# Output products of the state space part: the four summands in the outer loop, the four groups of 32 channels in the inner one

## The chip, the cores and the metric

The kernel runs on one core of a Trainium2 chip. The core has a matrix engine (TensorE, in the rows PE for the products and PEld for the loads of their stationary operand), a vector engine (VectorE, DVE), an activation engine (ScalarE, ACT), GpSimd (POOL) and SyncE (SP), whose queue starts the transfers from memory. Each engine runs its own list of instructions in order, and they meet through semaphores. PSUM, into which TensorE writes, has 8 banks of 128 partitions by 512 numbers of 32 bits. The metric is the device time of one execution in microseconds (us), as the median of several runs.

## What is computed

A layer with three mixers side by side (a diagonal state space part called S5, attention, retention), an output product, and then a layer of experts picked by keys. The change touches the end of the S5 part alone: the output `y`, a real product with the two halves of the complex state.

```python
def s5_mixer(u, lam_re, lam_im, log_dt, b_re, b_im, c_re, c_im, d_skip, w_glu):
    ...
    _, _, st_r, st_i = lax.associative_scan(_ssm_combine, (a_r, a_i, bu_r, bu_i), axis=1)
    y = (jnp.einsum('bsgp,ghp->bsgh', st_r, c_re.astype(jnp.float32))
         - jnp.einsum('bsgp,ghp->bsgh', st_i, c_im.astype(jnp.float32))
         + uf * d_skip.astype(jnp.float32).reshape(S5_NGROUPS, S5_GROUP))
    y = jax.nn.gelu(y.reshape(bsz, s, S5_CH))
    y = y * jax.nn.sigmoid(y @ w_glu.astype(jnp.float32))
    return y.astype(u.dtype)
```

There are 256 tokens (s), 16 groups (g) of 16 channels (h) with 64 states (p) each, so 256 channels and 1024 states. All numbers are of 32 bits.

## The kernel before

**Tiling of the S5 part.** Two groups with 64 states each fill the 128 partitions, so the 1024 states are 8 tiles `jj` of 128 states by 256 tokens. A tile feeds only its own 32 channels. Four tiles (`j` = 0 to 3) make up the 128 channels of one half `c` of the channels, and `c` runs over 0 and 1.

**The four summands.** The state of a tile is kept rotated: VectorE multiplies the two scanned arrays `zr` and `zi` with the cosines `pc` and the sines `pS`, and never adds the products up. So each tile has four arrays of 128 states by 256 tokens: `pc` (by then zr times cosine), `zi` (zi times sine), `xr` (zi times cosine) and `zr` (zr times sine). TensorE adds them up in PSUM by four products, with the real matrix `c_s[:, 0]`, its negative `c_neg[:, 0]`, and twice the negative of the imaginary one, `c_neg[:, 1]`.

**The products (line 521).** One product has a stationary operand of 128 states by 32 channels and a moving one of 128 states by 256 tokens. It writes 32 partitions of bank 6: partitions 32j to 32j + 31, columns 256c to 256c + 255. In the trace its form is "128*32 128x256". The four products of a tile accumulate on the same 32 partitions (`start` with the first, `stop` with the last). There are 2 by 4 by 4 = 32 of them. All operands are plain 32 bit numbers, and the trace has two records of every such product, so 64 records for these 32.

**Order before.** For each `c` the loop over `j` is outside and that over the four summands inside: four products in a row go to the same 32 partitions, then the next four go to the next 32.

**What stands around it in TensorE's list.** Ahead: the attention products at lines 500 and 509 and the last projection (`project(5, t)`, line 408). Behind: 8 transposes of the retention operands (line 530), 8 of the attention weights (line 538), the retention scores (551, 556), the gate's product (562) and more transposes and small products up to line 602. Then 16 products that only keep the engine busy (`keep_warm`, line 400), the transposes of the mixed result (392) and the output product by slices (426 to 428).

**Who waits for the end of line 521.** The last product sets `y_psum`, on which VectorE waits at line 911 (it adds the direct term), ScalarE's GELU (1254) stands behind that. ScalarE waits at line 1250 for the transposes of line 530, which stand behind line 521 in TensorE's own list. GpSimd has nothing to do until ScalarE has rounded the first slices of the output weights (1147), which comes after the whole mixing part.

**Other line for comparison.** `drive` (line 417) computes the inputs of the scans with products of another shape, "32*128 32x256": 32 partitions of input, 128 of output, a bank of its own for each `j`. There the loop over `j` is inside already.

Of the kernel before, what the change touches and what calls it, by code (L numbers as in the profile page):

```python
# [27 lines left out]
S = 256  # L28
# [87 lines left out]
def build(nc, x, w_in, vecs, consts, rots, decay, mask, s5_b, s5_c, w_glu, w_out, w_q, keys, u_t, v, out, spill):  # L116
    with ExitStack() as ctx:
# [24 lines left out]
        ps = ctx.enter_context(nc.psum_tensor("ps", [P, 8, 512], F32))  # L142
# [12 lines left out]
        def take(n):  # L155
            a = cursor[0]
            cursor[0] += n
            assert cursor[0] <= S * NKEY, cursor[0]
            return arena[:, a:a + n]
# [13 lines left out]
        pc = r3(take(S5_T * S), S5_T)  # L173
        zr, zi = (r3(take(S5_T * S), S5_T) for _ in range(2))
        squares = zr.rearrange("p j t -> p (j t)")
        xr = xn.rearrange("p t d -> p (t d)").rearrange("p (j t) -> p j t", j=S5_T)
# [30 lines left out]
        c_s = rawf[:, 2816:2816 + 512].rearrange("p (r j c) -> p r j c", r=2, j=S5_T)  # L207
        bb = rawf[:, 3328:3328 + 512].rearrange("p (r j c) -> p r j c", r=2, j=S5_T)
        c_neg = b_s
# [171 lines left out]
        def _(pe):  # L381
# [40 lines left out]
            def halves_product(dst, pairs, first, last):  # L422

                for i, (s_hi, s_lo, m_hi, m_lo) in enumerate(pairs):
                    end = last and i == len(pairs) - 1
                    pe.matmul(dst, s_hi, m_hi, start=first and i == 0, stop=False)  # L426
                    pe.matmul(dst, s_hi, m_lo, start=False, stop=False)  # L427
                    mm = pe.matmul(dst, s_lo, m_hi, start=False, stop=end)  # L428
                return mm
# [33 lines left out]
            for c in range(S5_C):  # L463
                for t in range(TT):
                    mm = pe.transpose(ps[:, 5, c * S + t * P:c * S + (t + 1) * P], u_tok[:, t, c * P:(c + 1) * P], ident)
            mm.then_inc(uT_psum, 1)
            pe.wait_ge(bb_ready, 1)
            for r in range(2):
                for c in range(S5_C):
                    mm = pe.transpose(ps[:, 6, (r * 2 + c) * P:(r * 2 + c + 1) * P],  # L470
                                      bb[:, r, 4 * c:4 * c + 4, :].rearrange("p j c -> p (j c)"), ident)
# [16 lines left out]
            for a in range(2):  # L488
                for h in range(4):
                    for t in range(TT):  # L490
                        mm = pe.transpose(ps[:, 4 + 2 * a + h // 2, (h % 2) * S + t * P:(h % 2) * S + (t + 1) * P],
                                          qk[:, t, a * MW + h * P:a * MW + (h + 1) * P], ident)
# [4 lines left out]
            for h in range(4):  # L497
                for o_ in range(2):
                    r = slice(HD * o_, HD * (o_ + 1))
                    mm = pe.matmul(ps[:, 4 + 2 * o_ + h // 2, (h % 2) * S:(h % 2 + 1) * S], mqT[r, h, P:S], mkT[r, h, :],  # L500
                                   start=True, stop=True)
# [4 lines left out]
            for h in range(4):  # L506
                for o_ in range(2):
                    r = slice(HD * o_, HD * (o_ + 1))
                    mm = pe.matmul(ps[:, 4 + o_, h * P:(h + 1) * P], mqT[r, h, 0:P], mkT[r, h, 0:P], start=True, stop=True)
# [3 lines left out]
            pe.wait_ge(c_ready, 1)  # L513
            for c in range(S5_C):
                pe.wait_ge(states_ready, c + 1)
                for j in range(4):
                    jj = 4 * c + j
                    parts = ((c_s[:, 0, jj, :], pc[:, jj]), (c_neg[:, 0, jj, :], zi[:, jj]),
                             (c_neg[:, 1, jj, :], xr[:, jj]), (c_neg[:, 1, jj, :], zr[:, jj]))
                    for n, (w, st) in enumerate(parts):  # L520
                        mm = pe.matmul(ps[32 * j:32 * j + 32, 6, c * S:(c + 1) * S], w, st,  # L521
                                       start=(n == 0), stop=(n == len(parts) - 1))
            mm.then_inc(y_psum, 1)

# [2 lines left out]
            for a in range(2):  # L527
                for h in range(2):
                    for t in range(TT):
                        mm = pe.transpose(ps[:, 2 + a, h * S + t * P:h * S + (t + 1) * P],  # L530
                                          ret[:, t, a * RW + h * P:a * RW + (h + 1) * P], ident)
# [21 lines left out]
            for h in range(2):  # L553
                for o_ in range(2):
                    r = slice(HD * o_, HD * (o_ + 1))
                    mm = pe.matmul(ps[:, 2 + o_, h * P:(h + 1) * P], rkT[r, h, P:S], rqT[r, h, P:S], start=True, stop=True)
# [3 lines left out]
            for m in range(S5_C):  # L560
                for c in range(S5_C):
                    mm = pe.matmul(ps[:, 7, m * S:(m + 1) * S], glu_s[:, c, m * P:(m + 1) * P], uT[:, c, :],
                                   start=(c == 0), stop=(c == S5_C - 1))
# [3 lines left out]
            for t in range(TT):  # L567
                for c in range(S5_C):
                    mm = pe.transpose(ps[:, 6, t * S5_CH + c * P:t * S5_CH + (c + 1) * P], uT[:, c, t * P:(t + 1) * P], ident)
# [8 lines left out]
            for h in range(RH):  # L578
# [4 lines left out]
                mm = pe.matmul(o1, rP1[:, h, :], ret[:, 1, vc], start=False, stop=True)  # L583
# [7 lines left out]
            for h in range(MH):  # L591
                g = 4 * (h % 2) + h // 2
                c = slice(h * HD, (h + 1) * HD)
                mm = pe.matmul(ps[:, 4, c], att0[:, g // 4, g % 4, :], mv[:, 0, c], start=True, stop=True)
# [3 lines left out]
            for h in range(MH):  # L598
                g = 4 * (h % 2) + h // 2
                c = slice(h * HD, (h + 1) * HD)  # L600
                pe.matmul(ps[:, 5, c], att1[:, g, 0:P], mv[:, 0, c], start=True, stop=False)
                mm = pe.matmul(ps[:, 5, c], att1[:, g, P:S], mv[:, 1, c], start=False, stop=True)
# [6 lines left out]
            for n in range(2):  # L609
                for k in range(KC):  # L610
# [4 lines left out]
                    for t in range(TT):  # L615
                        r = slice(t * P, (t + 1) * P)
                        mm = halves_product(ps[:, 4 + 2 * n + t, :],
                                            [(h_hi[:, k, r], h_lo[:, k, r], w_hi[:, k % 4, :], w_lo[:, k % 4, :])],
                                            k == 0, k == KC - 1)
# [5 lines left out]
            for n in range(2):  # L625
                for k in range(KC):
# [4 lines left out]
                    for h in range(4):  # L631
                        c = slice(h * P, (h + 1) * P)
                        mm = halves_product(ps[:, 4 * (1 - n) + h, 0:S],
                                            [(w_hi[:, k % 4, c], w_lo[:, k % 4, c], h_hi[:, k, :], h_lo[:, k, :])],
                                            k == 0, k == KC - 1)
# [46 lines left out]
            for t in range(TT):  # L682
                for a in range(3):
                    mm = pe.transpose(ps[:, 4 + t, a * P:(a + 1) * P], rows[:, t, a, :], ident)
# [842 lines left out]
```

## Time and profile before

| | us |
|---|---|
| median of 3 runs | 970.44 |
| the three runs | 970.31, 970.44, 973.07 |
| the profiled execution, its own time | 970.3 |
| span in its trace | 968.5 |
| from the first record of line 521 to the first of line 530 | 8.10 |
| mean granted clock of TensorE | 0.986 |

The span runs from the first to the last instruction of the trace; the 1.8 us around it belong to the time of the run and not to the trace. Of an engine's busy time TensorE has 96%. The first 205 us hold the mixers and the projections, in which the engines take turns; the rest is the expert part, one loop over the up projections and one over the down projections.

### The profile page before, as it was taken

The page shows a single profiled execution, that of the slowest core. Times are in us where ns is not written, and L with a number is a line of the kernel's source. Part 1 is how long each engine was busy: PE and PEld are TensorE (multiplying, and loading weights), DVE is VectorE, ACT ScalarE, POOL GpSimd, SP SyncE. Part 2 cuts the span into 40 slices and gives each one's busy share as a digit, 9 for nine tenths or more (in the row PEclk, how much of TensorE's full clock was granted, in tenths as well). Part 3 has the DMA queues.
Part 4 walks back from the last instruction along what each step waited for, and adds up shares of the span by engine and source line. Part 5 has one row for each costly group of instructions (what it writes and reads, how often), then busy time and mean ns, then how long its engine had stood idle before and what let it go on. Part 6 is the DMA issues. An engine that isn't in the chain of part 4 may idle for free.

```text
span 968.5 us, 20031 instructions
## 1 busy us (share of the span) xinstructions
PE 926.8 (96%) x5920; PEld 828.8 (86%) x5920; DVE 692.5 (72%) x1496; ACT 528.8 (55%) x1044; POOL 447.8 (46%) x370
## 2 busy tenths in 40 slices
PE   5794999999999999999999999999999999999998
PEld 5553568899999999999999999988888888888886
DVE  7379534202999912688888887788888888888886
ACT  4622555555555455555555555655566555655553
POOL 1779606587888888777777777300000000000000
PEclk9897999999999999999999999999999999999999
DMA  9422222216666666565555555776767677777773
GB/s 332 160 104 87 87 87 90 108 45 217 200 231 225 230 230 208 206 199 194 193 196 194 200 190 194 234 245 239 247 238 243 231 246 236 248 238 244 243 234 134
DMA packets 67435, 191.45 MB, mean 198 GB/s; under 512 B 6480, under 2 KB 8272, under 8 KB 67408
## 3 DMA queue, kind: packets, MB, share of 16 engines
q1 hardware_dynamic: 67408, 191.11, 57.8%
q8 instruction: 15, 0.25, 0.1%
q14 instruction: 12, 0.10, 0.0%
HBM read 173.78 MB, written 17.30 MB: 197 GB/s over the span
## 4 chain that ended last, share of the span: by engine, by line
PE 70%; POOL 14%; issue 7%; DVE 5%; ACT 3%; DMA 0%; POOLq 0%; SPq 0%; DVEq 0%
PE ps L426 21%; PE ps L427 21%; PE ps L428 21%; POOL w_lo L1455 10%; PE ps L666 3%; POOL w_lo L1419 2%; DVE routing L737 2%; PE ps L408 1%; PE ps L521 1%; ACT w_hi L1147 1%; PE ps L392 1%; ACT h_hi L1154 0%; DMA xs<-in_x 0%; DVE small L737 0%; DVE route_t L737 0%
## 5 line engine op out<-in xcount | busy, mean ns | idle before, releaser
L1311 ACT ACTIVATE w_hi<-raw 128x512 fp32r<-128x512 f32 x512 | 308.4, 628 | 137.3 <-PE ps L428 136.2
L1455 POOL TENSOR_TENSOR w_lo<-raw,w_hi 128x512 fp32r<-128x512 f32 x256 | 327.0, 1298 | 81.2 <-ACT w_hi L1311 80.9
L426 PE MATMUL ps<-h_hi,w_hi 128*128 128x256 f32 x1088 | 308.5, 284 | 2.5 <-POOL w_lo L1455 1.1
L427 PE MATMUL ps<-h_lo,w_hi 128*128 128x256 f32 x1088 | 307.9, 283 | 0.0
L428 PE MATMUL ps<-h_hi,w_lo 128*128 128x256 f32 x1088 | 307.8, 283 | 0.0
L737 DVE TENSOR_TENSOR w_lo<-raw,w_hi 128x512 fp32r<-128x512 f32 x256 | 177.4, 693 | 56.9 <-ACT w_hi L1311 41.9
L426 PEld LDWEIGHTS ps<-h_hi,w_hi 128*128 128x128 f32 x1088 | 208.8, 192 | 3.3 <-POOL w_lo L1455 1.3
L427 PEld LDWEIGHTS ps<-h_lo,w_hi 128*128 128x128 f32 x1088 | 208.8, 192 | 0.0
L428 PEld LDWEIGHTS ps<-h_hi,w_lo 128*128 128x128 f32 x1088 | 208.8, 192 | 0.0
L426 PE MATMUL ps<-w_hi,hot_gate 128*128 128x512 f32 x512 | 199.2, 389 | 0.0
L427 PE MATMUL ps<-w_lo,hot_gate 128*128 128x512 f32 x512 | 199.2, 389 | 0.0
L428 PE MATMUL ps<-w_hi,hot_gate 128*128 128x512 f32 x512 | 199.2, 389 | 0.0
L1325 ACT ACTIVATE acts<-ps 128x256 f32<-128x256 f32 x128 | 49.0, 383 | 177.5 <-PE ps L428 177.4
L1419 POOL TENSOR_TENSOR w_lo<-routing,w_hi 128x512 fp32r<-128x512 f32 (+1 forms) x64 | 84.6, 1339 | 81.4 <-ACT w_hi L1147 79.4
L426 PEld LDWEIGHTS ps<-w_hi,hot_gate 128*128 128x128 f32 x512 | 96.1, 188 | 20.1
L427 PEld LDWEIGHTS ps<-w_lo,hot_gate 128*128 128x128 f32 x512 | 96.1, 188 | 19.9
L428 PEld LDWEIGHTS ps<-w_hi,hot_gate 128*128 128x128 f32 x512 | 96.1, 188 | 19.8
L1066 DVE SCALAR_TENSOR_TENSOR hot_gate<-ps,route_t 128x256 fp32r<-128x256 f32 x256 | 105.6, 474 | 0.0
L737 DVE TENSOR_TENSOR route_t<-acts,routing 128x256 f32<-128x256 f32 x128 | 81.3, 635 | 3.0 <-ACT acts L1325 2.1
L737 DVE TENSOR_TENSOR routing<-routing,ps 128x512 f32 (+2 forms) x66 | 48.6, 736 | 40.0 <-ACT routing L1331 40.0
L426 PE MATMUL ps<-w_hi,h_hi 128*128 128x512 f32 (+1 forms) x96 | 39.3, 409 | 18.2 <-POOL w_lo L1419 17.4
L737 DVE TENSOR_TENSOR hot_gate<-route_t,hot_gate 128x256 fp32r<-128x256 f32 x128 | 53.9, 421 | 3.4 <-ACT hot_gate L1369 3.4
(196 smaller groups left out, 885.2 us busy)
## 6 DMA issues: line engine op xcount, KB each, us to landing
raw<-in_u_t SPq DMA_DIRECT2D x128, 512.0 KB, 3.4
raw<-in_v SPq DMA_DIRECT2D x128, 512.0 KB, 3.4
act_spill<-acts SPq DMA_DIRECT2D x62, 256.0 KB, 2.1
acts<-act_spill SPq DMA_DIRECT2D x62, 256.0 KB, 3.4
routing<-in_w_in SPq DMA_DIRECT2D x5, 2048.0 KB, 9.3
routing<-in_w_out SPq DMA_DIRECT2D x2, 2048.0 KB, 8.2
routing<-in_w_q SPq DMA_DIRECT2D x2, 2048.0 KB, 7.7
xs<-in_x SPq DMA_DIRECT2D x2, 512.0 KB, 4.9
```

The source lines that it names most:

```text
L392: mm = pe.transpose(ps[:, k // 2, (k % 2) * S + t * P:(k % 2) * S + (t + 1) * P], src[:, t, k * P:(k + 1) * P], ident)
L408: mm = pe.matmul(ps[:, 2 * ((n - 1) % 2) + t, :], hT[:, k, t * P:(t + 1) * P], w[:, k, :], start=(k == 0), stop=(k == KC - 1))
L426: pe.matmul(dst, s_hi, m_hi, start=first and i == 0, stop=False)
L427: pe.matmul(dst, s_hi, m_lo, start=False, stop=False)
L428: mm = pe.matmul(dst, s_lo, m_hi, start=False, stop=end)
L666: mm = pe.matmul(ps[:, 4 + 2 * (s % 2) + q // 2, (q % 2) * 2 * NKEY:(q % 2 + 1) * 2 * NKEY], hot_j[:, s % 2, q, :], hot_gate[:, s % 2, q]. ...
L737: return V.tensor_tensor(out_, a, b, op)
L1066: ins = V.scalar_tensor_tensor(hot_gate[:, s % 2, q], iota_p.unsqueeze(1).to_broadcast([P, 2, NKEY]), route_t[:, 0, one], route_t[:, 2:4, ...
L1311: A.activation(w_hi[:, 2 * (s % 2) + h, :], raw[:, s, h * HALF:(h + 1) * HALF], ACT.Copy)\
L1325: A.activation(acts[:, s, :], ps[:, s % 2, 0:S], ACT.Gelu_apprx_tanh).then_inc(act_ready, 1)
L1419: G.tensor_tensor(w_lo[:, m % 4, 0:width], w_ring[n % W_SLOTS][:, k, 0:width], w_hi[:, m % 4, 0:width].bitcast(F32), ALU.subtract).then_in ...
L1455: G.tensor_tensor(w_lo[:, slot, :], raw[:, s, h * HALF:(h + 1) * HALF], w_hi[:, slot, :].bitcast(F32), ALU.subtract).then_inc(lo_ready, 1)
```

## The change

The two loops inside `c` change places. The arrays are sliced by tile in the call and not ahead of it; operands, shapes, places in PSUM, flags, semaphores and the number of products are the same, and each output still adds up its four summands in the same order.

```diff
             for c in range(S5_C):
                 pe.wait_ge(states_ready, c + 1)
-                for j in range(4):
-                    jj = 4 * c + j
-                    parts = ((c_s[:, 0, jj, :], pc[:, jj]), (c_neg[:, 0, jj, :], zi[:, jj]),
-                             (c_neg[:, 1, jj, :], xr[:, jj]), (c_neg[:, 1, jj, :], zr[:, jj]))
-                    for n, (w, st) in enumerate(parts):
-                        mm = pe.matmul(ps[32 * j:32 * j + 32, 6, c * S:(c + 1) * S], w, st,
+                parts = ((c_s[:, 0], pc), (c_neg[:, 0], zi), (c_neg[:, 1], xr), (c_neg[:, 1], zr))
+                for n, (w, st) in enumerate(parts):
+                    for j in range(4):
+                        mm = pe.matmul(ps[32 * j:32 * j + 32, 6, c * S:(c + 1) * S], w[:, 4 * c + j, :], st[:, 4 * c + j],
                                        start=(n == 0), stop=(n == len(parts) - 1))
             mm.then_inc(y_psum, 1)
```

TensorE's list before, from the last projection to the transposes behind the S5 products (a name in brackets is a semaphore that the row waits for; xN is a count of rows alike):

```order
L408 MATMUL ps<-routing 128x512 [waits hT_ready,proj_ready,weights_in2]
L408 MATMUL ps<-routing 128x512 x7
L521 MATMUL ps<-routing,raw 32x256 [waits states_ready,c_negated]
L521 MATMUL ps<-routing,raw 32x256 x15
L521 MATMUL ps<-routing,raw 32x256 [waits states_ready]
L521 MATMUL ps<-routing,raw 32x256 x15
L530 MATMUL ps<-con,routing 128x128 [waits proj_ready,ret_rotated_ready]
```

The same place in the changed kernel, where the lines behind the edit are two lower:

```order
L408 MATMUL ps<-routing 128x512 [waits hT_ready,proj_ready,weights_in2]
L408 MATMUL ps<-routing 128x512 x7
L519 MATMUL ps<-routing,raw 32x256 [waits states_ready,c_negated]
L519 MATMUL ps<-routing,raw 32x256 x15
L519 MATMUL ps<-routing,raw 32x256 [waits states_ready]
L519 MATMUL ps<-routing,raw 32x256 x15
L528 MATMUL ps<-con,routing 128x128 [waits proj_ready,ret_rotated_ready]
```

Nothing moved between engines or across another line or wait. Only within each sixteen the order differs, which these rows don't show since all sixteen read alike: before, the 32 output partitions of `j` came 0 0 0 0 1 1 1 1 2 2 2 2 3 3 3 3, now 0 1 2 3 four times over.

## Rows read from the trace of the kernel before

**Rows 1.** Page, sections 1 and 2: busy time, then tenths per fortieth of the span.
```profile
PE 926.8 (96%) x5920; PEld 828.8 (86%) x5920; DVE 692.5 (72%) x1496; ACT 528.8 (55%) x1044; POOL 447.8 (46%) x370
PE   5794999999999999999999999999999999999998
PEclk9897999999999999999999999999999999999999
```

**Rows 2.** Chain that ended last, 104.7 to 134.2 us: start, us, what ended last.
```profile
104.80 1.93 PE ps L500 x16
106.73 7.06 PE ps L408 x16
113.79 1.09 PE ps L509 x16
114.88 7.06 PE ps L408 x16
121.95 8.10 PE ps L521 x64
130.04 1.04 PE ps L530 x8
...
131.11 0.60 ACT routing L1250
```

**Rows 3.** Line 521: records, ns shortest/median/longest, first and last start; who waited.
```profile
L521 PEld LDWEIGHTS ps<-routing,raw x64: 106/110/110, 121.9 to 129.5; 128*32 128x32 f32 x64
L521 PE MATMUL ps<-routing,raw x64: 379/379/404, 121.9 to 129.7; 128*32 128x256 f32 x64
...
  DVE routing L911: 12.5, 1
```

**Rows 4.** Timeline, loads of line 521: start, us, count; the first four of one tile.
```profile
121.88 0.11 PEld L521 LDWEIGHTS ps<-routing,raw 128*32 128x32 f32 x1 [0.76 <-issue]
122.12 0.11 PEld L521 LDWEIGHTS ps<-routing,raw 128*32 128x32 f32 x1
122.33 0.11 PEld L521 LDWEIGHTS ps<-routing,raw 128*32 128x32 f32 x1
122.55 0.11 PEld L521 LDWEIGHTS ps<-routing,raw 128*32 128x32 f32 x1
```

**Rows 5.** The same timeline a little later: loads that overlap are merged.
```profile
122.77 0.11 PEld L521 LDWEIGHTS ps<-routing,raw 128*32 128x32 f32 x2
122.98 0.14 PEld L521 LDWEIGHTS ps<-routing,raw 128*32 128x32 f32 x2
123.20 0.14 PEld L521 LDWEIGHTS ps<-routing,raw 128*32 128x32 f32 x2
```

**Rows 6.** Line 417 (`j` inside already), first drive: start, us, what, count.
```profile
45.72 0.31 PEld L417 LDWEIGHTS ps<-routing,raw 32*128 32x128 f32 x8 [0.35 <-issue]
46.04 0.20 PEld L417 LDWEIGHTS ps<-routing,raw 32*128 32x128 f32 x4
46.26 0.20 PEld L417 LDWEIGHTS ps<-routing,raw 32*128 32x128 f32 x4
```

**Rows 7.** Waits from 121 to 131 us; timeline behind line 521.
```profile
DVE routing L911 <- PE ps L521: 12.5, 1, 12.5
...
129.98 0.33 PE L530 MATMUL ps<-con,routing 128*128 128x128 f32 x1
```

**Rows 8.** Timeline from 104 us: what ScalarE and GpSimd wait for.
```profile
113.91 0.74 POOL L1407 TENSOR_TENSOR routing<-routing 128x256 f32<-128x256 f32 x1
121.98 0.69 ACT L1210 ACTIVATE routing<-ps,small 128x512 f32<-128x512 f32 x1 [1.22 <-PE ps L408]
131.11 0.60 ACT L1250 ACTIVATE routing<-ps 128x512 f32<-128x512 f32 x1 [8.44 <-PE ps L530]
```

**Rows 9.** Windows: PE, PEld, DVE, ACT, POOL busy, granted clock, DMA share, GB/s.
```profile
81.30:84.70 3.40, 1.42 (x7) 0.84 (x5) 3.37 (x3) 1.26 (x2) 3.32 (x3) 1.00 0.87 329
84.70:98.35 13.65, 3.39 (x17) 3.42 (x17) 13.44 (x15) 0.00 (x0) 13.41 (x15) 0.50 0.00 0
125.70:129.10 3.40, 3.40 (x33) 2.02 (x30) 0.00 (x0) 0.00 (x0) 0.00 (x0) 1.00 0.98 369
135.90:139.30 3.40, 1.78 (x16) 1.51 (x15) 1.47 (x3) 3.36 (x5) 0.00 (x0) 1.00 0.00 0
```

## The prediction

> **What bounds the kernel now.** I read the page first: TensorE is busy 96% of the span and no other engine is near it [rows 1], so a shorter stretch of TensorE can count, if it is one that everything waits for. The chain that ended last says whether it is. Between 104.8 and 130.0 us it is nothing but TensorE, line after line, and the 64 records of line 521 are 8.10 us of it (121.95 to 130.04); behind them come the transposes of line 530 and then ScalarE's copy at line 1250 [rows 2]. Then I asked who stands still meanwhile. VectorE waits 12.5 us for line 521 [rows 7]. ScalarE ends its last piece at 121.98 + 0.69 = 122.67 us and waits 8.44 us for line 530 (it starts at 131.11), and GpSimd's last piece ended at 113.91 + 0.74 = 114.65 us [rows 8]. Over 125.7 to 129.1 us VectorE, ScalarE and GpSimd are at 0.00 busy [rows 9]. What line 530 waits for besides its place in the list, the rotated retention operands, is GpSimd's piece of 114.65 us. So nothing lies beside line 521 that would be late next, down to 122.67 us, and what it loses the rest of the kernel gets, as long as the rest runs as before.
>
> **How the 8.10 us come about.** The first loads of line 521 start at 121.88, 122.12, 122.33 and 122.55 us [rows 4]: 0.24 us after the first record of a tile, then 0.216 (a record of 256 columns). Those all go to the 32 output partitions of j = 0. At 122.77 us two loads start at once, and from then on loads come in pairs 0.03 us apart, a new pair after 0.215 us (122.98, 123.20), each pair over in 0.14 us [rows 5]. I read the second of a pair as that of j = 1, whose products start while those of j = 0 still run. One stream of 8 tiles with 8 records each would need 64 x 0.216 = 13.8 us; it took 8.10, so on average 13.8 / 8.10 = 1.7 groups of 32 partitions were at work at a time. With four products in a row for each group, only neighbours meet: the second half of one with the first half of the next.
>
> **The change, part by part.** It removes, adds and moves nothing but the order within each sixteen products; waits, records and places are the same.
>
> *What it costs in each group:* for one j there are 4 summands x 2 records x 2 halves c = 16 records. They have to follow each other at 0.216 us, since they accumulate on the same partitions, as before.
>
> *What goes away:* now four neighbouring products have four different j. Nothing of the trace shows four groups of output partitions at once. The nearest rows are two. One is line 521 itself, where two ran together and neither became slower (0.215 us from pair to pair, as for one alone) [rows 5]. The other is line 417, four groups of input partitions with j inside: 8 loads in 0.31 us, then 4 at 46.04 and 4 at 46.26 us, so four streams side by side with 0.22 us to a round, and the fourth load only 0.02 us behind the first (0.20 us for four loads of 0.18) [rows 6]. Bounds: at best all four run freely, 16 rounds; at worst they take turns. I take the first end, because line 521 already shows the same kind of stream twice at no cost, and line 417 that TensorE's list can feed four.
>
> *The sum:* first gap 0.24, 14 more of 0.216 = 3.02, so the last round starts 3.26 us after the first; 0.02 for the fourth stream; then as now to line 530: the last record of line 521 starts 0.3 us before it (129.7 against 129.98 [rows 3, 7]). Together 3.6 us in place of 8.10, a gain of **4.5 us**.
>
> *Both halves c.* The second half waits for states that VectorE had finished long before: it idles for 12.5 us up to the end of line 521, 130.04, so it was done at about 117.5 [rows 2, 7]. No new wait.
>
> *Feeding the list.* Four streams take a record every 0.054 us, where line 521 now takes one every 0.127 (8.10 / 64). While the projection runs for 7.06 us [rows 2] the products behind it can queue up, and line 417 took records at that rate, though only 16 of them [rows 6]. If the list ran dry and the second half went at the rate of now, it would take 32 x 0.127 = 4.1 us instead of 1.8, and the gain would be 2.2 us. That is the price of the cover being too short.
>
> *What then comes earlier.* Everything from line 530 on moves by the gain. The transfer of 2 MB that starts at 122 us (0.98 of the DMA engines, 369 GB/s up to 129) now runs beside transposes and ScalarE copies that came after it. Beside that same transfer line 521 did 30 loads in 3.4 us [rows 9], 0.113 us each, no slower than its mean, so I cost this at nothing. The profiled execution of before took 970.3 us around a span of 968.5, and the median is 970.44, so both stand for the same state; 970.4 less 4.5 is **965.9 us**.
>
> A rule of the Trainium skill speaks against this sum. "TensorE: Matmul & The Clock Gate", part 3 (Packing small matmuls), says that a weight load overlaps products in flight only where the two have different row groups; here all tiles use the same 128 rows. By that, line 521 would have no two streams, and the change could gain nothing. The trace disagrees already: loads of 0.11 us start at 122.12 and 122.33 us while records of 0.379 us run, and the round still is 0.216 us [rows 3 to 5]. The same part gives 2.38 times for three column tiles, an estimate by which the 13.8 us of records would be 5.8 us for three and less for four; it names the gain, but with another width.
>
> **Rivals.**
> - *Loads take turns* (that rule, as a mechanism of this kernel): each of the four loads of a round, 0.11 us, stops all streams. A round is 0.216 + 4 x 0.11 = 0.66 us, 16 of them 10.5, with 0.3 behind them 10.8 us: **973.1 us**, slower. Against it: rows 4 and 5, where loads cost nothing.
> - *A drain at each change of group.* Between line 408 and 521, or 521 and 530, TensorE changes its form and loses about 0.1 us (0.3 to the next record where 0.216 is usual). If every change of j cost that and kept streams apart, the 32 products would take 0.24 + 0.31 us each, 17.6 us in all: 9.5 us more, **979.9 us**. This decides as soon as a product costs over 8.10 / 32 = 0.253 us. For it: before, there are only 7 changes of j, now 31. Against: the changes that are there start 0.006 to 0.03 us after the record before [rows 5], no drain. I give both of these 4% together.
> - *Two streams at most.* What the trace shows is two. Then 32 rounds of 0.216 + 0.3 = 7.2 us, a gain of 0.9: **969.5 us**. Reading the moving operands could be the limit: four streams of 128 partitions read four times what line 417 reads. 8%, with the case that the order in the list isn't what sets the overlap.
> - *Three, or a list that runs dry:* 64 / 3 rounds + 0.3 = 4.9 us, a gain of 3.2 us, or 2.2 by the sum above: **967.2 to 968.2 us**. 10%.
> - *The clock.* TensorE's granted clock fell from 2.4 to 1.2 GHz at 84.7 us, after a stretch of 3.4 us with TensorE at 1.42 us busy, and stayed there for 13.65 us; with 1.78 of 3.4 us busy, in 135.9 to 139.3, it stayed at 2.4 [rows 9]. That thin stretch stays as it is, but comes 4.5 us earlier and closer behind the projection, with a shorter S5 part between. If the clock fell there for as long as at 84.7, TensorE's work would take up to 13.65 / 2 = 6.8 us more: 965.9 to **972.7 us**. 5%.
>
> **How the numbers follow.** Full overlap 73%, three streams or a dry list 10%, two streams or no effect 8%, the clock 5%, turns or drains 4%. The likeliest gives 965.9 us. For the range, the full case has some tenths of its own (the runs of before differ by 0.1 us, with one at +2.6), which sets 964.7 below. Above, it has to take in the three streams and the two, so 969.7; what lies outside is most of the clock's case and the slower ones, and runs that scatter. A measurement of this kernel can tell about 0.3% (2.9 us) from no change: faster then means under 967.5. That is the full case, a part of the three streams and little of the clock: 0.78. Slower, above 973.3, is the drain: 0.03. The rest is 0.19.
>
> **What would show it.** In the profile of the changed kernel the products should take about 3.6 us from their first record to the first transpose, with loads in fours every 0.216 us; VectorE's wait for them should be 8.0 instead of 12.5 us, and ScalarE's for line 530 3.9 instead of 8.4. Rounds of 0.43 us would say two streams, 0.29 three, 0.66 loads that take turns. Rounds of 0.216 first and slower ones in the second half would say that the list ran dry. If the products are that short and the time isn't 4.5 us lower, the windows from 130 to 205 us tell where it went: a granted clock of 0.50 in them, or a wait that was not there. The forecast is wrong if four streams of 128 partitions can't be read at once, which no row shows.

## The result: 965.9 us, and the 4.5 us are where they were looked for

The changed kernel takes 965.89 us (median of 6 runs, 965.31 to 966.08) against 970.40 (median of 6) for the kernel before. The ratio is 0.9946, with a 95% interval of 0.9931 to 0.9960: a gain of 0.4 to 0.7%. The profiled execution took 965.99 us around a span of 964.2, so 1.8 us lie around the span, as before.

The page of the changed kernel, sections 1 and 2, answers to [rows 1]:

```profile
PE 922.8 (96%) x5920; PEld 826.6 (86%) x5920; DVE 692.5 (72%) x1496; ACT 528.6 (55%) x1044; POOL 447.8 (46%) x370
PE   5794999999999999999999999999999999999998
PEclk9797999999999999999999999999999999999999
```

TensorE's products are busy for 4.0 us less and its loads for 2.2 us less; the other engines differ by 0.2 us at most. The chain that ended last, from 104.9 to 134 us (start, us, what ended last), answers to [rows 2]:

```profile
104.99 1.93 PE ps L500 x16
106.92 7.06 PE ps L408 x16
113.98 1.09 PE ps L509 x16
115.08 7.07 PE ps L408 x16
122.14 3.59 PE ps L519 x64
125.73 1.04 PE ps L528 x8
126.77 0.02 issue
126.79 0.60 ACT routing L1248
```

Each piece has its length of before, but for line 519 (521 before): 3.59 us in place of 8.10. What the line is made of, and the loads in the timeline (loads that overlap are merged, with their count), answer to [rows 3 to 5]:

```profile
L519 PEld LDWEIGHTS ps<-routing,raw x64: 106/110/111, 122.1 to 125.1; 128*32 128x32 f32 x64
L519 PE MATMUL ps<-routing,raw x64: 378/379/403, 122.1 to 125.4; 128*32 128x256 f32 x64
```

```profile
122.31 0.13 PEld L519 LDWEIGHTS ps<-routing,raw 128*32 128x32 f32 x4
122.53 0.13 PEld L519 LDWEIGHTS ps<-routing,raw 128*32 128x32 f32 x4
122.74 0.13 PEld L519 LDWEIGHTS ps<-routing,raw 128*32 128x32 f32 x4
```

A record is as long as before (0.379 us, of which the end is modelled by the profile, so the starts count for more), a round is 0.216 us as before, but now a round holds four loads, all within 0.13 us where one takes 0.11. Four streams of 128 partitions run side by side and none is slower for it.

Who waited, and for how long (engine and line, what it waited for, us in all, times, longest), answers to [rows 7, 8]:

```profile
DVE routing L909 <- PE ps L519: 8.1, 1, 8.1
...
ACT routing L1248 <- PE ps L528: 3.9, 1, 3.9
```

The span fell by 4.3 us and not by 4.5. The first piece of the chain, the transfer of the input, is the reason; the rows are the first of the chain from 0 to 36 us, of the kernel before and of the changed one:

```profile
1.67 4.50 DMA xs<-in_x
```

```profile
2.14 5.70 DMA xs<-in_x
```

It ended 1.7 us later (7.84 against 6.17), and of that 0.19 us were left where the mixers' last products begin: line 500 began at 104.99 against 104.80, and 4.51 - 0.19 = 4.32 us, which is the 968.5 - 964.2 of the spans. Behind line 519 nothing is given back: from there to the end of the loops the records of TensorE stand 4.30 to 4.32 us earlier all along.

### The profile page after: what moved, and what is told of

It reads as the page before. It is cut to its first block, busy times and chain, and to the rows that moved or that the text cites. A ratio compares the mean times of both kernels' runs of the same rounds, so it can differ in the third digit from the quotient of the medians.

```text
span 964.2 us, 20031 instructions
## 1 busy us (share of the span) xinstructions
PE 922.8 (96%) x5920; PEld 826.6 (86%) x5920; DVE 692.5 (72%) x1496; ACT 528.6 (55%) x1044; POOL 447.8 (46%) x370
## 4 chain that ended last, share of the span: by engine, by line
PE 70%; POOL 14%; issue 7%; DVE 5%; ACT 3%; DMA 1%; POOLq 0%; SPq 0%; DVEq 0%
PE ps L426 21%; PE ps L428 21%; PE ps L427 21%; POOL w_lo L1453 10%; PE ps L664 3%; POOL w_lo L1417 2%; DVE routing L735 2%; PE ps L408 1%; DMA xs<-in_x 1%; ACT w_hi L1145 1%; ACT h_hi L1152 0%; PE ps L519 0%; DVE small L735 0%; DVE route_t L735 0%; POOL routing L1437 0%
```

## Experiments

The question that the result leaves is why the old order had 1.7 groups at work, and what in general decides. The theory was formed on [rows 4, 5]: j = 1 began 0.89 us after j = 0, four records or two products later, so when the third product of j = 0 began to run and only its fourth was left to wait. So: TensorE takes products in the order of the list; each group of 32 output columns holds two of them, one that runs and one that waits; the first product that finds its group full holds up all behind it, of whatever group. All numbers below are of the stretch from the first product to the first transpose behind, as the chain gives it; the kernel before has 8.10 us there and the changed one 3.59. Each kernel computes the reference's outputs in full. The diffs are against the changed kernel, whose two loops go out in each of them but the last; `...` stands for lines left out, such as the product's call with the operands and places of before.

**Two summands of a group in a row.**

```diff
-                for n, (w, st) in enumerate(parts):
-                    for j in range(4):
+                for n, j in [(2 * a + b, j) for a in range(2) for j in range(4) for b in range(2)]:
+                    w, st = parts[n]
...
```

> The same 32 products, but two summands of one group of 32 channels in a row before the next group comes: 0 0 1 1 2 2 3 3, twice for each half. Theory: the matrix engine takes products in the order of its list, and a group of 32 output columns holds two of them, one that runs and one that waits; the first that finds its group full stops the list. Then two in a row are free, all four groups run at once, and the stretch up to the transposes is 3.6 us as with the new order, 966 us in all. Rival: a group only starts when its predecessor has half of its block behind it, so two streams at a time whatever the length of a block: 7.5 us and about 970 us.

The chain of this kernel:

```profile
125.10 3.66 PE ps L519 x64
```

3.66 us, and 966.08 us in all (median of 8; ratio 0.9951, 0.9938 to 0.9964). So it isn't needed that neighbours differ. The rival, by which this would have stayed with two streams (7.5 us), is out. So is a limit on how far ahead of the oldest unfinished product TensorE looks, whatever the group: the order of before would put it at three products (j = 1, the fifth, began with the third), and here the first product of j = 3 is the seventh in the list, and 3.66 us leave no room for it to wait. (The profiled execution of this kernel took 969.03 us; 3.0 us of it had been lost by 65.4 us, see the last section.)

**Three in a row, then one each.**

```diff
+                for n, j in [(n, j) for j in range(4) for n in range(3)] + [(3, j) for j in range(4)]:
...
```

> Three summands of a group in a row (000 111 222 333), then the fourth of each (0 1 2 3), for each half. Theory of two held per group: the third product stops the list for two records (0.43 us) in each block, and the stretch takes 5.3 to 5.5 us (worked out product by product with 0.216 us a record), 967.7 us in all. If a group held three products it would be 3.6 us, if one only 8.35 us. Rival of half a block: about 6.6 us.

```profile
121.72 5.51 PE ps L519 x64
```

and loads near its start (two places of the timeline; loads that overlap are merged, with their count):

```profile
121.65 0.14 PEld L519 LDWEIGHTS ps<-routing,raw 128*32 128x32 f32 x2 [0.76 <-issue]
...
122.11 0.14 PEld L519 LDWEIGHTS ps<-routing,raw 128*32 128x32 f32 x3
```

5.51 us for an expected 5.3 to 5.5, and 967.89 us in all (median of 5). At 122.11, 0.46 us after the start, three loads come at once: I read them as the next of j = 0 and the first two of j = 1. So the second group came in two records after the first here, and four records after it in the old order (0.89 us), in both when all products of j = 0 but the waiting one had begun. The third product in a row is the one that costs: a group that held three would have given 3.6 us, one that held one 8.35, and the rival of half a block 6.6. This run names the number two, and the old order agrees: counted in the same way, 0.216 us a record, it would take 10.9 us with one held and 4.8 with three, and it took 8.10.

**The new order in the first half of the channels only.**

```diff
+                order = [(n, j) for n in range(4) for j in range(4)] if c == 0 else [(n, j) for j in range(4) for n in range(4)]
+                for n, j in order:
...
```

> The new order for the first half of the channels, the order of before for the second. Theory of two held per group: 6.2 to 6.4 us for the stretch (16 us records of the second half staggered as before), so 1.8 us less than before, 968.6 us. Not half of the gain (5.85 us, 968.1 us), because the old order's cost lies in its blocks being staggered one behind the other and its last block is short of company in either kernel. Rival: the time is a sum of two independent halves, 5.85 us.

```profile
125.02 6.25 PE ps L520 x64
```

6.25 us for 6.2 to 6.4 by the theory, and 5.85 by a sum of two halves; 968.84 us in all (median of 10; ratio 0.9982, 0.9970 to 0.9994). Half of the edit brings 1.85 of the 4.51 us, as the last block of the old order ends alone in either kernel.

**Groups in pairs.**

```diff
+                for n, j in [(n, 2 * a + b) for a in range(2) for n in range(4) for b in range(2)]:
...
```

> Groups in pairs: all four summands for groups 0 and 1 by turns, then for groups 2 and 3, for each half. Theory of two held per group: the second pair starts once the fourth summand of the first pair is accepted, four records (0.86 us) after its start, so 4.5 to 4.7 us for the stretch and 966.9 us in all. Rival, two streams at most at any time by the hardware: 7.2 us, 969.5 us (this fell already with the changed kernel, which had four).

```profile
125.09 4.55 PE ps L519 x64
```

4.55 us for 4.5 to 4.7; 967.20 us in all. With this, six orders of the same 32 products gave 8.10, 6.25, 5.51, 4.55, 3.66 and 3.59 us, each within some 0.2 us of what the rule of two gives product by product (7.9, 6.2, 5.3, 4.5, 3.6, 3.6). What the rule lacks in the old order fits the first gap of a block, 0.24 us in place of 0.216 [rows 4], which is paid anew by each block. One thing these runs can't tell: every product is two records, so "two products" may as well be "four records".

**Four times the work.** This is for the step on which the prediction had least: whether the list can feed four streams once what queued up behind the projection is used.

```diff
-                for n, (w, st) in enumerate(parts):
-                    for j in range(4):
+                for n, j in [(n, j) for _ in range(4) for n in range(4) for j in range(4)]:
+                    w, st = parts[n]
...
```

> The new order with each sixteen products done four times over, the last time's result counting (128 products, 256 records). Theory, the list feeds four streams for as long as it must: 64 rounds of 0.216 us, 14.0 us for the stretch, 10.4 us more than the changed kernel, 976.3 us. Rival, the list runs dry once what queued up behind the projection is used: rounds longer than 0.216 us from some place on, at the old rate of 0.127 us a record up to 30 us for the stretch.

```profile
122.01 13.95 PE ps L519 x256
```

13.95 us, so 64 rounds of 0.216 us: in the trace each round starts 0.215 or 0.216 us after the one before (0.24 for the first), so 256 records at one in 0.054 us. The list never ran dry. The whole took 978.27 us (2 runs) and not 976.3: 2 us more than the stretch explains, which appear at the very end.

**Twice the loads for the same columns.** This is for the loads.

```diff
-                for n, (w, st) in enumerate(parts):
-                    for j in range(4):
...
+                for h in range(2):
+                    for n, (w, st) in enumerate(parts):
+                        for j in range(4):
+                            mm = pe.matmul(ps[32 * j:32 * j + 32, 6, c * S + h * P:c * S + (h + 1) * P], w[:, 4 * c + j, :],
+                                           st[:, 4 * c + j, h * P:(h + 1) * P], start=(n == 0), stop=(n == len(parts) - 1))
```

> The new order with each product cut in two of 128 tokens (64 products, 128 records of 128 columns), so twice the weight loads for the same columns. Theory: loads of the four groups overlap each other and the records in flight, and a round of four is the greater of 0.109 us of columns and 0.11 us of one load; 32 rounds, 3.6 to 3.9 us for the stretch, 966 to 966.3 us. Rival, the four loads of a round take turns: 0.44 us a round, 14 us and 976 us. Rival, feeding: each record costs the list 0.05 us or more, so a round is 0.2 us and the stretch 6.7 us.

The chain, and the window of its first 3.42 us (PE, PEld, DVE, ACT, POOL busy, clock, DMA share, GB/s):

```profile
121.88 3.63 PE ps L520 x128
```

```profile
121.88:125.30 3.42, 3.42 (x128) 3.36 (x128) 0.00 (x0) 0.69 (x1) 0.00 (x0) 1.00 0.69 199
```

3.63 us: 128 loads of 0.11 us, 14.1 us of loading one by one, fit into it, so on average four at a time. So loads of different column groups overlap each other and the records in flight, though all use the same 128 rows. The list feeds a record every 0.028 us here. Both rivals, turns (14 us) and feeding (6.7 us), are out. In all it took 968.06 us, 2.2 more than the changed kernel, and again none of it in the stretch or behind it up to the last product. The transfers in the last 8 us (queue 8 brings in instructions; the row of `out` ends with the median us to landing) show where, this kernel first:

```profile
q8 instruction: 1, 0.02, 0.8%
issues: line engine op xcount, KB each, median us to landing
out<-xs SPq DMA_DIRECT2D x4, 256.0 KB, 2.6
```

The changed kernel over the same stretch:

```profile
issues: line engine op xcount, KB each, median us to landing
out<-xs SPq DMA_DIRECT2D x4, 256.0 KB, 2.1
```

Here the slowest of the four output transfers landed after 4.1 us, in the changed kernel after 2.1. The kernel with four times the work has the same two signs: its slowest output transfer took 4.1 us, with one piece of instructions brought in beside it. That the one delays the other is what the rows suggest; it wasn't tried apart.

**The transposes ahead of the products.** In the changed kernel ScalarE still waits 3.9 us for line 528. Here the block of 8 transposes with its two waits stands ahead of the products.

```diff
+            pe.wait_ge(ret_rot_ready, 1)
+            pe.wait_ge(proj_ready, 8)
+            for a in range(2):
+                ...
+            mm.then_inc(retT_psum, 1)
+
             pe.wait_ge(c_ready, 1)
             for c in range(S5_C):
...
```

The same lines are taken out behind the products.

> The new order, and the 8 transposes of the retention operands moved ahead of the 32 products. Theory: ScalarE, which waits 3.9 us for them in the changed kernel, does its two copies (1.1 us) beside the products, and they leave the chain; the products end 1.04 us later, so VectorE's sum starts 1.04 us later, and the GELU starts 1.3 to 0.3 us earlier, according to whether its table load waits for that sum. 964.6 to 965.6 us. Rival: the table load and the sum take the copies' place and nothing is gained, 965.9 us.

ScalarE in its timeline:

```profile
125.34 0.60 ACT L1249 ACTIVATE routing<-ps 128x512 f32<-128x512 f32 x1 [0.18 <-PE ps L518]
125.83 0.59 ACT L1250 ACTIVATE routing<-ps 128x512 f32<-128x512 f32 x1
126.44 1.28 ACT L1253 ACT_TABLE_LOAD   x1
129.87 0.63 ACT L1253 ACTIVATE routing<-routing 128x512 f32<-128x512 f32 x1 [2.14 <-DVE routing L910]
...
133.39 0.60 ACT L1262 ACTIVATE route_t<-ps 128x512 f32<-128x512 f32 x1 [0.61 <-PE ps L561]
```

Both copies and the table load of 1.28 us now stand beside the products, and the GELU waits for VectorE's sum alone. It began 5.44 us after the end of the projection (129.87 - 124.43) and not 7.05 (129.19 - 122.14), 1.6 us earlier where 0.3 to 1.3 were expected; 0.6 of this went again in front of line 1262, which waits for TensorE. From the end of the projection to the table load at line 1136, which stands on the chain of both, it is 12.57 us (124.43 to 137.00) against 13.58 (122.14 to 135.72 at line 1135) in the changed kernel: 1.0 us less. The median was 964.91 us (5 runs). Since its interval overlapped that of the changed kernel, the two ran once more beside each other.

> The changed kernel itself once more, on the same chip as the version with the transposes ahead, since the two differ by 1 us in medians from different jobs and their intervals overlap: 965.9 us, 3.6 us for the stretch.

> The version with the transposes ahead of the products, beside the changed kernel. In the trace the GELU began 5.6 us after the first of the two groups of lines instead of 7.1, and 0.4 us of that was given back behind it, so 1.0 us less than the changed kernel: 964.9 us. Rival, what was seen was the difference of two jobs: 965.9 us.

The changed kernel: 965.85 us (10 runs, 965.4 to 969.5). This version: 966.04 us (6 runs, 964.57 to 968.76; ratio to before 0.9940, 0.9918 to 0.9961, against 0.9951, 0.9936 to 0.9967). The lowest three were 964.57, 964.90 and 965.10 against 965.40, 965.59 and 965.76, so the traces show 1.0 us less in this part, and the lowest runs agree. But three of the six runs lie 2 to 4 us above the others (the one of them that was profiled has the early stall of the last section), and the medians don't settle that the version is faster.

## The prediction, step by step

- **The stretch is alone on the path.** Right. All 4.5 us arrived behind it; VectorE waits 8.1 us (8.0 forecast) and ScalarE 3.9 (3.9).
- **Four streams at 0.216 us a round, 3.6 us.** Right: 3.59, term by term: the last round starts 3.26 us after the first, as summed. The open point was whether four moving operands of 128 partitions can be read at once. They can.
- **The overlap of before is 1.7 groups because only neighbours meet.** The number was right, and so was the place of j = 1's start, but "only neighbours meet" describes one order and isn't the rule. The rule that the six orders bear out is two products held per group in a list taken in order. [Rows 4, 5] are narrow views that cut the merged loads short: a wider one has two loads at 121.88 us (0.03 apart) and three from 122.77 on, of which I read the first as the sixth of j = 0 and the others as the first two of j = 1. The readings drawn from them stand.
- **The list feeds four streams.** Right, and with more room than claimed: the cover of the 7.06 us projection isn't needed to explain it, as 256 records in a row went at the full rate.
- **Loads cost nothing.** Right. The rule of the Trainium skill ("TensorE: Matmul & The Clock Gate", part 3, Packing small matmuls) that a load overlaps products in flight only when its row group is another doesn't hold here: the round stayed 0.216 us with four loads in it, and 0.109 with four loads of 0.11. The same part also lets a load into a background weight buffer come ahead of products in flight; no run here tells whether it is that. Its 2.38 times for three column tiles is of the same kind as what was seen: 13.8 / 3.59 = 3.8 times for four streams, where the 13.8 us of one stream are worked out and were not run.
- **What comes earlier runs beside the transfer, at no cost.** Right: the transposes took 1.04 us and the copies 0.60, as before, with the DMA engines busy all the time (from 125.7 to 129.1 us, at 394 GB/s).
- **Two streams or three, or a drain at a change of group.** Neither: the loads come in fours every 0.216 us, and the records of four groups follow each other 0.007 us apart.
- **The clock.** It did not fall in the thin stretch, which moved to 131.4 us. The granted clock stood at 1.00 there with 1.78 us of TensorE in 3.4, the same as [rows 9] have (columns as there: PE, PEld, DVE, ACT, POOL busy, clock, DMA share, GB/s):

```profile
131.40:134.80 3.40, 1.78 (x15) 1.38 (x14) 1.49 (x3) 3.36 (x5) 0.00 (x0) 1.00 0.00 0
```

- **965.9 us.** Measured: 965.89. The stretch is right by its mechanism; that the whole agrees to 0.01 us is luck, since the input transfer alone moved the start by 0.19 us and the six runs lie between 965.31 and 966.08.

## What to carry to other kernels

Where products are narrow (32 of 128 output columns here, numbers of 32 bits, two records each), put the loop over the column groups innermost, or at least let no more than two products in a row go to the same group: the third stops the whole list until the first has ended. An order can be costed by hand with that rule and the length of one record, to 0.2 us in this kernel. Then look at what only waits for its place in the same list: here 8 transposes, whose readers had nothing else to do.

## What was not expected of the hardware

- **Four full-height streams cost no more than one.** A round is 0.216 us with one, two or four groups, and beside a transfer of 2 MB.
- **A long program can pay at the end.** With 128 or 384 records more in TensorE's part (two kernels) the slowest of the four output transfers took 4.1 us to land and not 2.1, with a piece of instructions brought in beside it.
- **An early stall of 3 us.** In some executions a product of VectorE of the S5 part (line 735, 128x1024) takes 4.2 us in place of 1.7. TensorE then idles, and its clock falls. GpSimd's operations beside it (four on line 1417, merged), VectorE's, and two windows, of the two-in-a-row kernel:

```profile
49.92 5.05 POOL L1417 TENSOR_TENSOR w_lo<-routing,w_hi 128x512 fp32r<-128x512 f32 x4
51.87 4.19 DVE L735 TENSOR_TENSOR routing<-routing,route_t 128x1024 f32<-128x1024 f32 x1
```

```profile
58.00:61.40 3.40, 0.57 (x3) 0.49 (x4) 0.89 (x3) 1.25 (x3) 1.89 (x2) 1.00 0.00 0
61.40:64.80 3.40, 3.40 (x10) 2.66 (x8) 0.00 (x0) 0.00 (x0) 3.32 (x4) 0.50 0.47 117
```

And the changed kernel at the same operations:

```profile
49.91 7.00 POOL L1417 TENSOR_TENSOR w_lo<-routing,w_hi 128x512 fp32r<-128x512 f32 x4
51.85 1.71 DVE L735 TENSOR_TENSOR routing<-routing,route_t 128x1024 f32<-128x1024 f32 x1
```

These operations of VectorE and GpSimd take turns, and what differs is who goes first. In the changed kernel their operations end one after the other (GpSimd 52.47, VectorE 53.55, GpSimd 54.70, VectorE 55.78, GpSimd 56.92 us). In the two-in-a-row kernel GpSimd's two next operations, at 1.3 us each and not 2.3, go ahead of VectorE's, which ends 1.08 us behind them (54.98 and 56.06 us). All eleven profiled executions are of these two kinds: VectorE's operation takes 4.2 us where GpSimd's four take 5.05 together (five executions, of four kernels), and 1.7 us where they take 7.0 (six). What decides the turn stays open.

On VectorE this costs 1.4 us (line 838 begins at 57.23 us and not at 55.81). The other 1.6 of the 3.0 us come from TensorE: it stood idle for 3.58 us before GpSimd's next piece, and after 0.57 us of products in 3.4 the granted clock was 0.50 (1.2 GHz) for the next 3.4 us, where products of 512 columns followed each other at 0.43 us and not 0.23. In the changed kernel TensorE has 2.59 us of products in the same 3.4 us, and the clock stays at 1.00. Single runs 3 us over the rest occur with the kernel before too (973.07 us among its first three).
